# Values stationary and turned weights moving in two attention layers, and position columns as a third group of the compression matmuls

## The reference

```
o_c = einsum(p_c, v_cmp);  o_s = einsum(p_s, vg);  o_w = einsum(softmax(s_w), vw)
return gb[0] * o_c + gb[1] * o_s + gb[2] * o_w
flat = (blocks + pos_emb).reshape(B, G, n, CMP_BLOCK * d)
return gelu(flat @ w1) @ w2            # the compressed keys and values
```

## Time and profile before

| | |
|---|---|
| median of 3 runs | 1352.95 us (1350.23 to 1356.22) |
| the profiled execution: its own time | 1355.25 us |
| the profiled execution: span from first to last instruction | 1353.4 us |
| PE busy | 1322.7 us (98%), mean granted clock 0.988 of full speed |
| POOL, ACT, DVE busy | 1033.4, 717.9 and 383.1 us |
| stage 0 (up to the next stage's first product) | about 0 to 171 us |
| stage 6 | about 1031 to 1151 us |

### The profile page before, as it was taken

The page is one execution under the profiler, slowest core; times in us unless marked ns, Lnnn a source line. Parts: engine busy times, 40 slices in busy tenths (PEclk is TensorE's granted clock), DMA queues, the critical chain, the costliest instruction groups (busy, mean ns, idle before and its releaser), DMA issues.

```text
span 1353.4 us, 19562 instructions
## 1 busy us (share of the span) xinstructions
PE 1322.7 (98%) x7558; PEld 1094.3 (81%) x7558; DVE 383.1 (28%) x812; ACT 717.9 (53%) x1259; POOL 1033.4 (76%) x875
## 2 busy tenths in 40 slices
PE   7999999999989999999999998999999999999997
PEld 6988788888877887888887887888887888788886
DVE  2264321111266553111105555111103333301102
ACT  6554564454587786444444664544434564444531
POOL 7345888887984486888888777688889976788874
PEclk9799999999999999999999999999999999999999
DMA  8332565665653254666565545555665644466652
GB/s 276 109 95 84 166 190 183 188 190 176 197 159 95 75 154 127 203 188 182 181 189 170 175 140 147 182 187 184 187 186 188 202 155 140 142 216 187 196 171 84
DMA packets 63116, 224.91 MB, mean 166 GB/s; under 512 B 7344, under 2 KB 7984, under 8 KB 63024
## 3 DMA queue, kind: packets, MB, share of 16 engines
q1 hardware_dynamic: 62736, 223.57, 53.2%
q10 hardware_dynamic: 288, 0.10, 0.0%
HBM read 222.59 MB, written 1.05 MB: 165 GB/s over the span
## 4 chain that ended last, share of the span: by engine, by line
PE 93%; ACT 2%; POOL 2%; DMA 1%; DVE 1%; issue 0%; SPq 0%; ACTq 0%; DVEq 0%
PE G L1050 27%; PE G L1051 26%; PE G L1057 26%; POOL wlo L2193 2%; PE A L1224 2%; PE A L1081 1%; PE A L1159 1%; DMA raw<-in_w_e 1%; PE G L1224 1%; PE A L1195 1%; ACT whi L1926 1%; PE A L1071 1%; PE G L1159 1%; PE A L1093 0%; PE A L1357 0%
## 5 line engine op out<-in xcount | busy, mean ns | idle before, releaser
L2193 POOL TENSOR_TENSOR wlo<-raw,whi 128x256 fp32r<-128x256 f32 (+1 forms) x867 | 1023.8, 1220 | 302.0 <-ACT whi L1926 301.7
L1926 ACT ACTIVATE whi<-raw 128x1024 fp32r<-128x1024 f32 x403 | 425.9, 1059 | 339.4 <-PE G L1057 320.1
L1050 PE MATMUL G<-whi,xh 128*128 128x512 f32 (+2 forms) x1200 | 463.9, 390 | 11.2 <-DVE xl L1405 8.9
L1051 PE MATMUL G<-whi,xl 128*128 128x512 f32 (+2 forms) x1200 | 451.2, 380 | 0.0
L1057 PE MATMUL G<-wlo,xh 128*128 128x512 f32 (+2 forms) x1200 | 352.7, 380 | 0.8 <-POOL wlo L2193 0.8
L1050 PEld LDWEIGHTS G<-whi,xh 128*128 128x128 f32 x1200 | 227.3, 189 | 55.0 <-issue 14.4
L1051 PEld LDWEIGHTS G<-whi,xl 128*128 128x128 f32 x1200 | 228.1, 190 | 37.5
L1057 PEld LDWEIGHTS G<-wlo,xh 128*128 128x128 f32 x1200 | 219.4, 189 | 45.8 <-POOL wlo L2193 2.7
L1050 PE MATMUL G<-whi,hh 128*128 128x512 f32 x352 | 139.5, 396 | 0.0
L1051 PE MATMUL G<-whi,hl 128*128 128x512 f32 x352 | 138.9, 394 | 0.0
L1057 PE MATMUL G<-wlo,hh 128*128 128x512 f32 x352 | 110.4, 395 | 0.0
(11 more groups left out here) (349 smaller groups left out, 1196.1 us busy)
## 6 DMA issues: line engine op xcount, KB each, us to landing
raw<-in_g SPq DMA_DIRECT2D x88, 512.0 KB, 3.9
raw<-in_u SPq DMA_DIRECT2D x88, 512.0 KB, 4.0
raw<-in_d SPq DMA_DIRECT2D x88, 512.0 KB, 4.1
raw<-in_w_h SPq DMA_DIRECT2D x32, 512.0 KB, 3.7
raw<-in_w_e SPq DMA_DIRECT2D x24, 512.0 KB, 4.1
raw<-in_w_a SPq DMA_DIRECT2D x24, 512.0 KB, 3.7
raw<-in_w_b SPq DMA_DIRECT2D x24, 512.0 KB, 3.8
raw<-in_w_eo SPq DMA_DIRECT2D x8, 512.0 KB, 3.6
```

The source lines that it names most:

```text
L1050: e.matmul(o, sh[:, kt, xs], whi[h][:, ws], start=u.first and j == 0, stop=False)
L1051: e.matmul(o, sl[:, kt, xs], whi[h][:, ws], start=False, stop=False)
L1926: e.activation(whi[c % NH][:, 0:n], raw[c % NR][:, 0:n], ACT.Copy).then_inc(s_hi, 1)
L2193: m = e.tensor_tensor(wlo[c % NH][:, i:j], raw[c % NR][:, i:j], whi[c % NH][:, i:j].bitcast(F), ALU.subtract)
```

## The change

1. **AV is turned round** for stages 0 and 6. The 64 value columns of a head are stationary and the turned weights move. In stage 0, where two heads share their values, one matmul moves 2 x 128 columns; in stage 6 it moves 128. The output is turned already: heads of parity g land in partitions 64g to 64g + 63, and the matmuls of g = 0 and g = 1 alternate.
2. **The weights are normed before they are turned.** The new step NW (DVE) computes reciprocal sums (times gates in stage 0) and multiplies the weights with them from PSUM into `W`; TR waits for NW, not for EX. EX of stages 0 and 6 writes back into PSUM. The old NO shrinks to a copy or an add (branches 0 and 1); branch 2 is added by NA into the PSUM tile. WH (ACT) and WL (DVE), one pair for each token half, write `mh` and `ml`. MT, MH and ML are gone for the attention half of stage 0 and for all of stage 6. RC of stage 6 is gone.
3. **Compression.** `Z` has a third group with the position embedding in every 2nd of 32 columns, written once by DVE in MB. The 16 matmuls of a kind move 45 columns, and the 16 one-column matmuls are gone. Small gelu temporaries move to PSUM.
4. **Retention gate.** GU is gone. GS reads the projection from `G[0]`, so the wide product's first unit of each half waits for GS too. R8 multiplies by the sigmoid and by the raw gate, in two operations of 512 columns where there were four of 128. One small copy in R6 is gone.
5. **The plan.** Stage 0 from unit 18 and all of stage 6 are ordered anew; stage 4 has one TR a unit later.

```diff
-19: CPA 1 0 0; CG 0; CE 1; AV 1 0 0; CD 1; SC 1 0 1 @0; CF 1; MK 1 0 1
...
-29: CPA 1 1 0; NO 0 0 1; AV 1 1 0; RO 0 1; MT 0 @0; SC 1 1 1 @1
...
-57: GU 1; R8 0; R8 1; MT 2 @0
+18: MK 1 0 0; CA 0 @0; CA 1 @1; CB 0; CE 0; CD 0
+19: CB 1; CF 0
...
+25: NW 1 0 1; TR 1 0 0
+26: CPA 1 0 0; RO 0 0; AV 1 0 0; TR 1 0 1; NO 1 0 0
...
+53: EV 6 1
+54: GS 1
+55: GT 1
+56: R8 0
+57: R8 1; MT 2 @1
...
 compress_in:
-                for m in range(16):
-                    z = Z[:, 2 * kind:2 * kind + 2, 2 * m:2 * m + 225:16]
-                    e.matmul(tile[0:64, 0:30]..., wt, z, start=m == 0, stop=m == 15)
-                for m in range(16):
-                    pos = CP[:, (POSV if kind else POSK) + m:...+ 1]
-                    o = e.matmul(tile[0:64, 512:513], wt, pos, start=m == 0, stop=m == 15)
+                    z = Z[:, 3 * kind:3 * kind + 3, 2 * m:2 * m + 225:16]
+                    o = e.matmul(tile[0:64, 0:45]..., wt, z, start=m == 0, stop=m == 15)
...
 weighted, old:
-                for i in range(n):
-                    for b in range(nb):
-                        at = (i * nb + b) * 128
-                        m = e.matmul(tile[:, ow * i:ow * i + ow], w[1][0:kp, at:at + 128], vs[i][b],
-                                     start=b == 0, stop=b == nb - 1)
 weighted, new (stage 0, then stage 6):
+                    for b in range(nb):
+                        for g in range(2):
+                            m = e.matmul(heads4(tile[64 * g:64 * g + 64, 0:256], 2), v, wt[:, g:4:2, b, :], start=b == 0,
+                                         stop=b == nb - 1, skip_group_check=True)
+                    for j, b, g in itertools.product(range(2), range(nb), range(2)):
+                        m = e.matmul(tile[64 * g:64 * g + 64, 128 * j:128 * j + 128], v, wt[:, 2 * j + g, b, :],
+                                     start=b == 0, stop=b == nb - 1, skip_group_check=True)
...
 norm_weights (NW), new; the gates only in stage 0:
+                e.wait_ge(S["EX"], nth("EX", *key))
+                e.reciprocal(rs[key], sm[key])
+                e.tensor_tensor(gr[key], rs[key], gates[:, at:at + 4], ALU.mult)
+                e.tensor_tensor(s, ps, by, ALU.mult).then_inc(S["NW"], 1)
 turned_hi (WH), turned_lo (WL), new:
+                e.activation(mh[:, 2 * p:2 * p + 2, 128 * t:128 * t + 128], heads4(tile[:, 0:256], 2), ACT.Copy)
+                e.tensor_tensor(ml[...], heads4(tile[:, 0:256], 2), mh[...].bitcast(F), ALU.subtract)
 product, wide, stage 0:
+                        if u.st == 0:
+                            e.wait_ge(S["GS"], nth("GS", 0, u.t))
```

More of the change, by code:

```diff
@@ L616 @@
 10: MK 0 1; EX 0 0
[L617 to L624, removed]
+12: EV 1 0; NW 0 0; EX 0 1; LB 2
+13: TR 0 0; NW 0 1
+14: CPA 0 0
+15: AV 0 0; TR 0 1; EV 1 1; WH 0 0; CPA 0 1
+16: CPV 0 1; WL 0 0; AV 0 1
+17: WH 0 1; WL 0 1
+20: EV 2 0
+21: TBM 2
 23: EV 2 1
-24: KT 1 @1
-25: KV 1; KA 1; SC 1 0 @2; SC 1 1 @0; MK 1 0
+24: KT 1 @0
+25: KV 1; KA 1; SC 1 0 @1; SC 1 1 @2; MK 1 0
 26: MK 1 1; EX 1 0
[L629 to L641, removed]
+28: EV 3 0; NW 1 0; EX 1 1; LB 3
+29: TR 1 0; NW 1 1
+30: CPA 1 0
+31: AV 1 0; TR 1 1; WH 1 0; EV 3 1; CPA 1 1
+32: WL 1 0; CPV 1 1; AV 1 1; KT 2 @0; WH 1 1; WL 1 1
+33: KA 2; KV 2; SC 2 0 @1; SC 2 1 @2; MK 2 0
+34: MK 2 1; EX 2 0
+35: TBM 3
+36: EV 4 0; NW 2 0; EX 2 1
+37: TR 2 0; NW 2 1
+38: CPA 2 0
+39: TR 2 1; EV 4 1; CPA 2 1
+40: CPV 2 1; KT 3 @0
+41: KV 3; KA 3; SC 3 0 @0
 42: MK 3 0
 43: EX 3 0
[L644 to L651, removed]
+44: EV 5 0; NW 3 0
+45: AV 2 0; TR 3 0
+46: WH 2 0; CPA 3 0; WL 2 0
+47: AV 3 0; EV 5 1; SC 3 1 @1; WH 3 0; AV 2 1; WL 3 0; MK 3 1
+48: WH 2 1
+49: WL 2 1; EX 3 1
+51: NW 3 1
+52: TR 3 1
+53: CPV 3 1; CPA 3 1; AV 3 1
+54: WH 3 1; WL 3 1
 59: RES 0 0; BN 0 0
@@ L856, in program @@
         ret_st, ret_mv = [small(24) for _ in range(2)], [small(8) for _ in range(2)]
-        ret_va, ret_r = [small(4) for _ in range(2)], [small(4) for _ in range(2)]
+        ret_r = [small(4) for _ in range(2)]
         out_ms, out_r = [small(4) for _ in range(4)], [small(4) for _ in range(4)]
@@ L896, in mixed_sources, with turned @@
             if st == 0:
-                return [("NO", (0, br, p, t)) for br in range(3) for t in range(2)] if p < 2 else [("R8", (0, p - 2))]
+                return [("R8", (0, p - 2))]
             if st == 2:
                 return [("O3", (2, p))]
-            return [("NF" if st == 4 else "NO", (st, p, t)) for t in range(2)]
+            return [("NF", (st, p, t)) for t in range(2)]
+        def turned(st, p, t):
+            return (0, 2, p, t) if st == 0 and p < 2 else (6, p, t) if st == 6 else None
         def heads_by_level(kq, ps):
@@ L1031, in product @@
                             e.wait_ge(S["HL"], nth("HL", u.st, kt // 4, u.t))
-                if wide and u.st % 2 == 0 and u.bank == 0 and u.t == 0:
-                    e.wait_ge(S["ML"], nth("ML", u.st, u.kts[0] // 2))
+                if wide and u.st % 2 == 0 and u.bank == 0:
+                    of = turned(u.st, u.kts[0] // 2, u.t)
+                    if of:
+                        e.wait_ge(S["WL"], nth("WL", *of))
+                    elif u.t == 0:
+                        e.wait_ge(S["ML"], nth("ML", u.st, u.kts[0] // 2))
                 if u.first:
@@ L1515, in mask_short @@
                     e.wait_ge(s_unit, BEGIN[st])
+                else:
+                    e.wait_ge(d_cp, 16)
+                    e.memset(Z[:, 2:6:3, :], 0.0).then_inc(s_dve, dv.up())
+                    own()
+                    for kind, at_pos in enumerate((POSK, POSV)):
+                        e.tensor_copy(Z[:, 3 * kind + 2, 0:32:2], CP[:, at_pos:at_pos + 16])
                 e.tensor_copy(one[:, :], ident)
@@ L2024, in gelu_exp @@
             def gelu_exp(key):
[L2025 to L2026 removed]
+                tile, _ = lane_of("CA", key)
+                u = tile[0:64, 64:94]
                 e.wait_ge(S["CB"], nth("CB", *key))
```

267 lines of the change are left out of this document (142 added, 125 removed), and 2 rows, old and new, of the table SIGNALS.

## The result

The changed kernel takes 1331.95 us (median of 4 runs, 1330.26 to 1333.48), against 1353.38 us for the kernel before in the same measurement (4 runs, 1350.23 to 1356.22). The ratio is 0.984, with a 95% interval of 0.9816 to 0.9863. The forecast was 1333.5 us. The profiled execution took 1333.37 us, with a span of 1331.6 us.

The account below looks back on a forecast made before the run. PE time was taken as the bound, busy 98% of the span. Terms 8.3 + 5.5 + 2.8 + 3.4 - 0.5 = 19.5 us took the span from 1353.4 to 1333.9 us, median 1333.5 us; range 1324 to 1338 us, chance 0.67.

Parts of the forecast that it names:

- 1. Compression: Stage 0's small matmuls: one-column ones go and less runs at half clock, -8.3 us.
- I take one short fall like that after R8's wait: Compression: the still sparse run brings about 3.4 us at half speed, giving 1.7 us of the gain back.
- the full 10.0 us: Compression: the gain if the clock does not fall, one-column matmuls gone and the rest at full clock.
- 15 more columns I cost at nothing: Compression matmuls going from 30 to 45 columns: no added time, with a bound of 0.8 us in all.
- The 75 ns of a one-column matmul: Compression: 75 ns for one column against 62 ns for 30, taken to show that columns do not set the time.
- 2 and 3. AV and MT: Stages 0 and 6: AV turned round in overlapping pairs, -5.5 us; the transposes MT gone, -2.8 us.
- 20 exits of 0.15 us: Stages 0 and 6: leaving each turned AV call costs 0.15 us more than before, 20 times.
- the interruptions of the products: Six interruptions of products go with MT: 0.2 us for all, each worth from nothing to 0.15 us.
- The first rival: AV in stages 0 and 6: the pairs do not overlap, +2.0 us instead of -5.5, 1341 us; chance 0.12.
- 4. Tail of the retention: End of stage 0: PE's 2.03 us wait for R8 and the slow clock behind it go, -3.4 us.
- 5. NW: NW on DVE before TR in stages 0 and 6: hidden by the plan, 0 us, 0.5 us allowed.
- The rival of the turned chain: PE waits for NW at TR in all 20 keys, slow clock behind longer waits, 1359.5 to 1366 us; chance 0.04.

Follow-up runs that it names:

- experiment 2: Kernel before with the compression's third group, and CF and the steps around it set one or two units apart: 1346.1 us, ratio 0.9952.
- experiment 3: Changed kernel with the 32 one-column compression matmuls put back, their result unread: 1339.21 us, ratio 0.9896.
- experiment 1: Kernel before with only the third group of the compression (45 columns, no one-column matmuls), old order: 1350.41 us, ratio 0.9981.
- experiment 5: Changed kernel with both groups of AV written to the lower 64 partitions, so no pair uses two array halves: 1342.12 us, ratio 0.9921.
- Experiment 8: Kernel before with only the retention gate's change (GU gone, GS from PSUM, R8 in two wide operations, EV 6 1 after unit 53): 1350.95 us, ratio 0.9985.
- experiment 7: Changed kernel with NW's large multiplication on DVE done twice, 1331.69 us, or four times, 1360.97 us.
- experiment 6: Changed kernel with AV's matmuls ordered all lower half first, then all upper half, not alternating: 1333.95 us, ratio 0.9863.
- NW four times: Changed kernel with NW's large multiplication on DVE made four times: 1360.97 us, ratio 1.0061.
- NW twice: Changed kernel with NW's large multiplication on DVE done twice, to the same place: 1331.69 us, ratio 0.9845.
- experiment 9: Changed kernel with GS reading the evicted gate from SBUF and the wide product not waiting for GS: 1330.44 us, ratio 0.983.
- experiment 4: Changed kernel with compression reading 30 columns 16 apart, 45 consecutive, or three groups of 15 consecutive: 1328.55, 1329.4 and 1329.88 us.

## Why the prediction was right

The median came out 1.6 us under the forecast, the profiled span 2.3 us under it. The mechanisms of all five parts are the ones that work, but the sum is nearer than its terms. By the traces the edits took 22.3 us out of stages 0 and 6, against the 19.5 us forecast; a start that was 1.0 us longer in the trace after, and nothing of the change, brings the span closer to the forecast. By the parts of the prediction:

**1. Compression: forecast -8.3 us, measured -7.7 us** (experiment 2; -8.1 us when undone in experiment 3; both in units 18 to 53). The size is near because errors cancel. "I take one short fall like that after R8's wait" failed: the clock does not fall at all, which gives the full 10.0 us, 1.7 us more. "15 more columns I cost at nothing" failed too: 81 ns for 60 ns is 1.3 us, outside the bound of 0.8 us that I gave, because the bound came from consecutive columns and these lie 16 apart. PE's work outside the compression's matmuls became 2.0 us shorter in experiment 2 and not 2.7 us, and a wait of 0.3 us was added there. The 75 ns of a one-column matmul were misread: the clock falls inside that piece, at 43.7 us, and at full clock they take 57 ns (experiment 3). The conclusion from it, that so few columns don't set the time, stands. And one thing was not seen: what the values' matmuls covered. That the new plan sets CF a unit later looked like a detail of the order; without it 2.7 us of the gain are lost (experiment 1 against 2).

**2 and 3. AV and MT: forecast -5.5 and -2.8 us, together -8.3 us, measured -11.4 us.** Units 18 to 53 fell by 14.1 us; without the 7.7 us of the compression 6.4 us are left for AV and MT, and stage 6, where AV and MT are all there is to gain, fell by 5.0 us. AV's own instructions take 8.6 us in stage 0 and 6.5 us in stage 6, against 14.5 us (experiment 2, where none of them runs at half clock) and 10.3 us: 9.8 us less, where 8.5 us were forecast. Costing it like the paired scores was right, 0.05 to 0.06 us a call too dear. The 24 transposes took 2.6 us, as forecast. The term that was sized wrong is what the calls cost and give back around them: 20 exits of 0.15 us less 0.2 us for the interruptions of the products, 2.8 us in the forecast, is 1.0 us in the traces. An exit costs 0.15 us as I said, also before transposes (L1209 in the chain above), but in stage 6 one of the eight calls is followed by scores, at no cost, and all products together take 0.1 us less than before although three of them stand behind an AV. So the interruptions were likely priced too low; this is a difference of rows, and MT was not tried alone.

The first rival, pairs that do not overlap at 1341 us, is what experiment 5 built, at 1342.1 us. AV's own instructions take 27.0 us there, 2.2 us more than the old AV's 24.8 us; the rival had +2.0 us. Its price is about right, and it is not what the changed kernel does.

**4. Tail of the retention: forecast -3.4 us, measured -3.2 us** (from unit 54 on). From the start of the old wait to the end of the second MT it was 7.4 us (149.93 to 157.37 us) and is 3.7 us; the GS wait, forecast as 0.3 us, costs 0.4 us of idle and 0.2 us in the product behind it. Experiment 8 has the same step alone at -2.6 us, with 0.9 us for GS.

**5. NW: forecast 0 with 0.5 us allowed, measured 0.** The rival of the turned chain needs more than twice NW's time (experiment 7: 0.7 us lost with 17 us more, 29 us with 50 us more). It had its place, the line of TR, and the clock behind the waits right.

Stage 0 in sum: 7.7 + 6.4 + 3.2 = 17.3 us, against 17.95 us from the first product on. The other 0.6 us lie before unit 18: a wait at L1103, 0.6 us in the trace of the kernel before, is missing in the changed kernel, but in experiments 2 and 8 too, where the plan of those units is the old one. It belongs to the execution.

Open is the clock where no edit is. In stage 2 it varies without a pattern. Stage 7 takes 193.6 to 193.7 us in every kernel with the old attention, and 192.4 us in the changed one and in most of its variants, but 193.6 us again in those whose stage 6 was made slower (experiments 5, 6 and NW four times). So these 1.2 us went with the shorter stage 6 in every trace, and the prediction does not have them. But stage 5 lacks the same 1.2 us, and the slow stretch of 3.4 us at its start, in NW twice and in experiment 9, where nothing near it was edited. What decides is not shown.

## What to carry to other kernels

Before small work is taken off the bounding engine, ask what ran under it: here the values' one-column matmuls hid the end of the keys' gelu, and a third of the gain (2.7 of 7.7 us) hung on setting the consumer one unit later. Do not price a small matmul by its count of columns alone: here 45 close columns cost no more than 30, and 45 columns 16 apart cost a third more. A layout of `Z` with close columns would be worth up to 1.3 us; with the right values it was not tried. Matmuls with 64-column stationaries on the two halves of the array run two for about the time of one here, also with four instructions in a row to the same half, and with eight in a row half of that is lost. And read what an edit is worth from the piece where it acts: the start of the kernel alone moved by 1.1 us between traces, as much as several of the effects here.

## What the hardware showed that I had not expected

- 45 moving float32 columns 16 elements apart take 81 ns, 45 neighbouring ones 60 ns, 30 that are 16 apart 60 ns, one column 57 ns (64 stationary columns, experiments 3 and 4).
- PE overlaps halves of the array over a run of four instructions to one half and four to the other, without loss; at eight and eight it takes 1.51 us where alternating takes 1.02 us and one half alone 1.89 us.
- The granted clock falls while PE is busy without a gap, in the kernel before at 43.7 us, 3.0 us into the small matmuls, in experiment 3 at 46.9 us, 6.6 us into them; it stays at 1.00 through the 5.2 us of the changed kernel. So the length of the run before the fall does not explain it alone, as the expectation of experiment 1 has it; what does is open.
